# A norm's squares and the next projection's first weights, moved into the output projection ahead of it

## The chip, the cores and the metric

The kernel runs on one core of one Trainium2 chip, in one launch. The metric is the device time of the launch in microseconds. All arithmetic is in 32-bit floats; a large product is made from three matmuls over operands split into a rounded part and a rest.

## The reference, cut to what matters

The network is a block of two layers followed by a block of one layer with other branches. Every layer begins with a root-mean-square norm and a wide input projection, and its mixing part ends with an output projection added to the residual:

```python
def rms_norm(x, w):
    y = x * rsqrt(mean(x * x, axis=-1) + EPS)
    return y * w

for l in range(2):                         # first block
    h = rms_norm(x, norm_w[l]) * (1 + scale) + shift
    parts = split_in(h @ w_in[l])          # projection, then attention and two convolutions
    y = mixer_branches(parts, ...)
    x = x + gate * (y @ w_out[l])          # layer 0 also updates 256 context tokens
# second block
h = rms_norm(x, norm_mix) * (1 + scale_m) + shift_m
proj = h @ w_in                            # then Mamba, attention and gated delta branches
x = x + gate_m * (merged @ w_out)
x = x + gate_f * moe(...)
```

The model width is 1024; there are 1024 tokens and 256 context tokens (the context is dropped after the first block).

## The kernel before

The residual `k.x` stays in SBUF as 8 chunks of 128 channels (the partitions) by 1280 tokens (columns 0 to 255 are the context). `k.x_r` is the same memory, and so are `k.h` and `k.h_r`. Work is cut into stages; each ends in a barrier of all engines, and inside one the engines run their own instruction lists and wait on semaphores in them. There is no planner: the written order is the order.

An output projection is `project_residual` (L1391). It makes 8 output chunks in four groups of two, each chunk for each token block: 24 products in layer 0 (256, 512 and 512 tokens), 16 in layer 1 (512 and 512). SyncE loads the weights of a group (L1421) and the old residual from DRAM (L1430); GpSimd splits the weights of groups 1 to 3 (L1439, L1441); TensorE makes a product in 24 matmuls; VectorE adds it to `k.x` (L1516) and increments `added`, which lets TensorE use that PSUM bank in the next group. ScalarE has nothing to do after its roundings at the start (L1480, L1485).

The norm is `norm_steps` (L268), set beside the first pair of the next projection: `ring_gemm` (L392) in the first block, `delta_inputs` (L1603) behind it. It walks blocks of tokens: 512, 384 and 128 (`X_NORMS`), and in layer 1 the 256 context tokens last. SyncE loads two halves of 128 weight columns, 512 KB each (L248), then stores the residual to DRAM, one DMA for a block (L280). ScalarE squares the chunks of a block (L298), into four buffers; TensorE sums them over partitions and chunks with a matrix of ones (L287), 8 matmuls for a block; ScalarE takes Ln and Exp (L303, L307), which gives the inverse root; VectorE makes `k.h` from `k.x` (L344); ScalarE writes the rounded part over `k.x` (L314), and so waits first for the store of that block (`kept_in`); VectorE makes the rest (L350); TensorE takes the products with the two weight halves. Block 0's squares come first and those of block i + 1 are interleaved with the roundings of block i, likewise the sums between the products. The two weight halves are rounded by ScalarE (L255) and their rests made by VectorE (L262) ahead of the first block.

Products of the first pair: for the first 512 tokens both halves of the weights as each chunk arrives; for the other 512 the first half as the chunks of the 128-token block arrive, then the second half. A half of the next pair's weights is loaded when the last product that uses that half is done; ScalarE rounds it and GpSimd makes the rest (L262).

Ahead of layer 1's norm stands a small stage, `silu_columns` (L587). Ahead of the norm of `delta_inputs` there is none. Layer 0 has such a norm as well, and the mixing part's own projection in the second block is also a `project_residual`.

Of the kernel before, what the change touches and what calls it, by code (L numbers as in the profile page):

```python
# [269 lines left out]
def norm_steps(nc, k, s, norm, ring, tiles):  # L270
# [5 lines left out]
    last = len(blocks) - 1  # L276

# [4 lines left out]
    def sums(pe, i, j):  # L282
        n, w = i * DK + j, blocks[i][1]
        if i >= 2 and j == 0:
            pe.wait_ge(s.logged, i - 1)
        pe.wait_ge(s.squared, n + 1)
        nc.tensor.matmul(ps[i % 2][:, 0:w], k.ones[:, :], sq[n % 4][:, 0:w], start=j == 0, stop=j == DK - 1)\  # L287
            .then_inc(s.summed, 1)

    def scalar(act):  # L290
# [9 lines left out]
        def take_root(i):  # L300
            w = blocks[i][1]
            act.wait_ge(s.summed, (i + 1) * DK)
            nc.scalar.activation(lg[:, 0:w], ps[i % 2][:, 0:w], ACT.Ln, bias=k.eps, scale=1.0 / D).then_inc(s.logged, 1)  # L303
            act.wait_ge(s.logged, i + 1)
            if i >= 2:
                act.wait_ge(s.scaled, (i - 1) * DK)
            nc.scalar.activation(root[i % 2][:, 0:w], lg[:, 0:w], ACT.Exp, scale=-0.5).then_inc(s.rooted, 1)  # L307
# [23 lines left out]
    def vector(dve):  # L331
# [7 lines left out]
        for n in range(2):  # L339
            rest_half(nc, ring, dve, n)  # L340

        def scale(i, j):
            t0, w, which = blocks[i]
            nc.vector.scalar_tensor_tensor(k.h[:, j, t0:t0 + w], k.x[:, j, t0:t0 + w], factor[:, j, which:which + 1],  # L344
                                           root[i % 2][:, 0:w], ALU.mult, ALU.mult).then_inc(s.scaled, 1)
# [19 lines left out]
def norm_tiles(nc, es, norm):  # L365

    sq = norm.squares or [es.enter_context(sbuf(nc, f"rm_sq{i}", [P, 512], F32)) for i in range(4)]
    lg = es.enter_context(sbuf(nc, "rm_log", [P, 512], F32))
    root = [es.enter_context(sbuf(nc, f"rm_root{i}", [P, 512], F32)) for i in range(2)]
# [4 lines left out]
def ring_gemm(nc, k, name, ring, parts, blocks, then=None, extra=None, norm=None):  # L374
# [7 lines left out]
    with ExitStack() as es, stage(nc, names) as s, nc.Block() as block:  # L382
# [18 lines left out]
        def _(sp):  # L401
            if norm:
                for n in range(2):
# [23 lines left out]
        def _(pe):  # L427
# [963 lines left out]
def project_residual(nc, k, name, w, src, src_r, blocks, mod, gate_at, kept, sums=None):  # L1391
# [7 lines left out]
    names = "w_in0 w_in1 w_in2 w_in3 x_in0 x_in1 x_in2 x_in3 rounded rest w_rounded w_rest split products added summed biased"  # L1399

    with ExitStack() as es, stage(nc, names) as s, nc.Block() as block:
# [8 lines left out]
        early = DK // 2  # L1410

# [4 lines left out]
        def _(sp):  # L1416
            for g in range(n_pairs):
# [12 lines left out]
                sp.dma_start(k.x[:, pair, first:T1], kept[:, pair, first:T1]).then_inc(x_in[g], 16)  # L1430

        @block.gpsimd
        def _(pool):
            pool.wait_ge(s.rest, DK)
            for g in range(1, n_pairs):
                for c in range(2):
# [5 lines left out]
                                            ALU.subtract).then_inc(s.split, 1)  # L1442

# [33 lines left out]
        def _(act):  # L1477
# [8 lines left out]
            round_chunks(range(early, DK))  # L1486

        @block.vector
        def _(dve):
            def take_rests(chunks):  # L1490
                for j in chunks:
                    dve.wait_ge(s.rounded, j + 1)
                    nc.vector.tensor_tensor(src_r[:, j, :], src[:, j, :], k.h_r[:, j, 0:total].bitcast(F32),  # L1493
                                            ALU.subtract).then_inc(s.rest, 1)

# [12 lines left out]
            for g in range(n_pairs):  # L1508
                dve.wait_ge(x_in[g], 16)
                for t in range(per):  # L1510
# [6 lines left out]
                                                   ALU.mult, ALU.add).then_inc(s.added, 1)  # L1517

# [13 lines left out]
def first_block(nc, k, a):  # L1532
    with sbuf_views(nc, "branches", [P, DK, T1]) as (k.y, k.y_r):
        for l in range(2):
            first_layer(nc, k, a, l, l == 1)


def first_layer(nc, k, a, l, last):
# [7 lines left out]
    with ExitStack() as es, ExitStack() as conv:  # L1546
        ring = conv.enter_context(weight_ring(nc, f"ring{l}"))
# [4 lines left out]
                     weight=f"norm_w{l}", edges=edges, squares=None)  # L1552
# [7 lines left out]
        sums = attention(nc, k, a, l, last, cq, ckv, kr, ahead)  # L1560
    project_residual(nc, k, f"out{l}", a.w_out[l], k.y[:, :, blocks[0][0]:T1], k.y_r[:, :, blocks[0][0]:T1],
# [2332 lines left out]
```

## Time and profile before

| | us |
|---|---|
| median of 3 runs | 4379.31 (4378.44 to 4383.56) |
| the profiled execution | 4386.62 |
| its span | 4384.8 |
| TensorE busy | 3901.9 (89%) |
| VectorE busy | 2111.7 (48%) |
| ScalarE busy | 1575.0 (36%) |
| GpSimd busy | 617.0 (14%) |

The engines overlap, so the busy times don't add up to the span. Times of single events below count from the start of the span. The profiled execution is 7.3 us above the median. The output projection of layer 0 ends near 1137 us and layer 1's norm follows it; that of layer 1 ends near 2059 us, and the norm of `delta_inputs` follows it.

### The profile page before, as it was taken

The numbers are of one execution on the slowest core, as the hardware profiler recorded it, in microseconds if no ns is written. First come the engines' busy times: TensorE is split into PE (matmuls) and PEld (weight loads), VectorE is DVE, ScalarE is ACT, GpSimd is POOL, SyncE is SP. The second block draws the span as 40 slices with busy tenths as digits, with TensorE's granted clock in tenths as the row PEclk, the third lists the DMA queues.
The fourth block names the chain that finished last, engine by engine and source line by source line (L and its number), as shares of the span: only waits on it lengthen the run. The fifth ranks groups of instructions, "written<-read, shape, count | busy, mean of one in ns | idle before, by whom it ended". The sixth has DMA issues, their size and how long they took to land. (4 is left out here: it accounts for less than half of the span.)

```text
span 4384.8 us, 41863 instructions
## 1 busy us (share of the span) xinstructions
PE 3901.9 (89%) x16132; PEld 2780.2 (63%) x16132; DVE 2111.7 (48%) x2657; ACT 1575.0 (36%) x2450; POOL 617.0 (14%) x300
## 2 busy tenths in 40 slices
PE   4899799999899799999876889898999897999996
PEld 1687555558686455567655866576777675666664
DVE  0391366662373366651438423233343226666665
ACT  1412345541322245441452235522221114555552
POOL 0021200002021200001110011022333330111111
PEclk9999889998999799989888989999999997999997
DMA  4211100002211112122112211022233337999985
GB/s 173 77 39 32 36 15 29 29 29 91 68 44 41 31 53 63 58 80 93 30 20 68 49 40 20 10 72 78 82 94 77 89 121 257 360 352 353 354 293 211
DMA packets 339924, 450.95 MB, mean 103 GB/s; under 512 B 45149, under 2 KB 214418, under 8 KB 338194
## 3 DMA queue, kind: packets, MB, share of 16 engines
q1 hardware_dynamic: 325026, 405.30, 29.5%
q0 software_dynamic: 12112, 25.19, 1.6%
q10 hardware_dynamic: 2592, 17.83, 1.0%
q8 instruction: 128, 2.10, 0.2%
q14 instruction: 66, 0.54, 0.0%
HBM read 408.41 MB, written 59.24 MB: 107 GB/s over the span
## 5 line engine op out<-in xcount | busy, mean ns | idle before, releaser
L1140 PE MATMUL values<-probs,vp 128*128 128x512 f32 x672 | 349.0, 601 | 12.0 <-issue 6.4
L1228 ACT ACTIVATE probs<-scores 128x512 f32<-128x512 f32 (+1 forms) x336 | 196.0, 583 | 307.9 <-PE scores L220 306.2
L218 PE MATMUL scores<-q_hi,k_rest 97*128 97x512 f32 (+1 forms) x336 | 262.4, 781 | 0.0
L3555 PE MATMUL dp<-h_t,abt 128*128 128x512 f32 x544 | 241.9, 597 | 1.1 <-ACT abt L3604 0.9
L3586 ACT ACTIVATE expert_hi<-wu 128x1024 fp32r<-128x1024 f32 x136 | 144.8, 1065 | 250.6 <-PE gp L220 250.6
L1309 DVE TENSOR_REDUCE mx<-made 128x1 f32<-128x640 f32 (+1 forms) x272 | 203.9, 794 | 28.7 <-PE made L1081 27.9
L218 PE MATMUL gates_ps<-x_t_r,ring_r 128*128 128x512 f32 (+1 forms) x560 | 206.2, 368 | 2.6 <-PEq L84 2.6
L218 PE MATMUL smb<-x_t_r,merge_w_r 128*128 128x512 f32 x480 | 195.9, 408 | 13.9 <-POOL merge_w_r L2802 11.1
L730 DVE SCALAR_TENSOR_TENSOR conv_out<-conv_in,vectors,conv_out 128x1295 f32<-128x1295 f32 (+1 forms) x120 | 205.5, 1713 | 4.3
L219 PE MATMUL gates_ps<-h_t_r,ring_hi 128*128 128x512 f32 (+1 forms) x560 | 206.1, 368 | 0.0
L220 PE MATMUL gates_ps<-x_t_r,ring_hi 128*128 128x512 f32 (+1 forms) x560 | 206.0, 368 | 0.0
L3637 DVE TENSOR_TENSOR wu_r<-wu,expert_hi 128x1024 fp32r<-128x1024 f32 x136 | 166.4, 1225 | 74.3 <-ACT expert_hi L3586 71.4
L1439 POOL TENSOR_TENSOR out_hi<-out_w,ones 128x1024 fp32r<-128x1024 f32 x18 | 43.0, 2392 | 1076.9 <-DVE branches_r L1493 947.3
L220 PE MATMUL smb<-x_t_r,merge_hi 128*128 128x512 f32 x480 | 192.4, 401 | 0.0
L262 POOL TENSOR_TENSOR ring_r<-ring_w,ring_hi 128x1024 fp32r<-128x1024 f32 x40 | 104.9, 2623 | 550.1 <-ACT ring_hi L255 550.1
L218 PE MATMUL out_ps<-h_t_r,out_w_r 128*128 128x512 f32 (+1 forms) x448 | 171.1, 382 | 10.9 <-DVE out_w_r L1499 10.9
L3637 DVE TENSOR_TENSOR wg_r<-wg,expert_hi 128x1024 fp32r<-128x1024 f32 x136 | 165.7, 1225 | 21.1 <-ACT expert_hi L3586 13.4
L3555 PEld LDWEIGHTS dp<-h_t,abt 128*128 128x128 f32 x544 | 100.6, 190 | 117.6 <-issue 114.8
L3052 DVE TENSOR_TENSOR merge_sg<-smb,merge_sg 128x512 f32<-128x512 f32 x48 | 33.2, 692 | 287.1 <-PE smb L220 287.1
L220 PE MATMUL out_ps<-h_t_r,out_hi 128*128 128x512 f32 (+1 forms) x448 | 170.1, 380 | 0.0
L1516 DVE SCALAR_TENSOR_TENSOR x_t<-out_ps,mod,x_t 128x512 f32<-128x512 f32 (+1 forms) x56 | 39.1, 711 | 250.3 <-PE out_ps L220 250.2
L1140 PEld LDWEIGHTS values<-probs,vp 128*128 128x128 f32 x672 | 111.2, 190 | 74.9 <-issue 42.7
(572 smaller groups left out, 9525.9 us busy)
## 6 DMA issues: line engine op xcount, KB each, us to landing
wg<-in_w_gate SPq DMA_DIRECT2D x34, 2048.0 KB, 10.0
wu<-in_w_up SPq DMA_DIRECT2D x34, 2048.0 KB, 11.2
h_t<-in_w_down SPq DMA_DIRECT2D x34, 2048.0 KB, 9.7
ahead_w<-in_w_ada SPq DMA_DIRECT2D x48, 512.0 KB, 3.9
ring_w<-in_w_in SPq DMA_DIRECT2D x44, 512.0 KB, 4.1
mod_w<-in_w_mod ACTq DMA_DIRECT2D x8, 1536.0 KB, 29.2
ahead_w<-in_w_mod SPq DMA_DIRECT2D x24, 512.0 KB, 3.5
out_w<-in_w_out SPq DMA_DIRECT2D x24, 512.0 KB, 4.9
```

The lines of the kernel that those rows point to most:

```text
L218: nc.tensor.matmul(out, lhs[1], rhs[0], start=start, stop=False, **kw)
L219: nc.tensor.matmul(out, lhs[0], rhs[1], start=False, stop=False, **kw)
L220: return nc.tensor.matmul(out, lhs[0], rhs[0], start=False, stop=stop, **kw)
L262: eng.tensor_tensor(ring.rest[:, c, :, :], ring.w[:, c, :, :], ring.hi[:, c, :, :].bitcast(F32), ALU.subtract)\
L730: step(nc.vector.scalar_tensor_tensor(o, i, wt, o, ALU.mult, ALU.add))
L1140: nc.tensor.matmul(O[b % 2][:, 0:w], vp[g // 2 % 2][:, kb, g % 2 * VD:g % 2 * VD + P], pr[m % 3][:, 0:w], start=kb == 0, stop=kb == nk - 1 ...
L1228: nc.scalar.activation(pr[m % 3][:, 0:w], S[m % 2][:, 0:w], ACT.Exp, scale=scale).then_inc(s.exped, 1)
L1309: nc.vector.tensor_reduce(mx[:, p, j:j + 1], src, AX.X, ALU.max).then_inc(s.maxed, 1)
L1439: nc.gpsimd.tensor_tensor(hi[:, q, :, :], wt[:, q, :, :], all_ones(k), ALU.mult).then_inc(s.split, 1)
L3555: m = nc.tensor.matmul(dp[half][:, :], at[:, j, :], wd[u][:, j, half * 512:(half + 1) * 512], start=j == 0, stop=j == FK - 1)
L3586: nc.scalar.activation(w_hi[:, p % RING, :, :], weights(u, p, False), ACT.Copy).then_inc(s.w_hi, 1)
L3637: nc.vector.tensor_tensor(weights(u, p, True), weights(u, p, False), w_hi[:, p % RING, :, :].bitcast(F32), ALU.subtract).then_inc(s.w_rest, 1)
```

## The change

- `project_residual` gets `ahead` for the two layers of the first block: the weight ring of the next projection, its first columns, and a buffer `summed` of 128 by 1280 (5 KB a partition, at a fixed place). Behind its other DMAs SyncE loads the two first halves. After each `added`, ScalarE squares that piece of `k.x` and VectorE adds it to `summed`, one product later. ScalarE rounds the two halves ahead of the first square of the last group, and GpSimd makes their rests behind its other work.
- In the norms of layer 1 and of `delta_inputs`, one matmul with the ones for a token block takes the place of eight and of the squares; ScalarE takes all roots first, in buffers that hold every token; the loads, roundings and rests of the first two halves are gone from there.
- The ring is opened ahead of `project_residual` and closed where it was closed (in `delta_branch` for the last). Layer 0's norm and the third `project_residual` do what they did.

```diff
@@ norm_steps
+    summed, fresh = norm.summed, ring.halves == 0
+    sums_each = 1 if summed is not None else DK
...
+        if summed is not None:
+            if j == 0:
+                nc.tensor.matmul(ps[i % 2][:, 0:w], k.ones[:, :], summed[:, t0:t0 + w], start=True, stop=True)\
+                    .then_inc(s.summed, 1)
+            return
...
+            act.wait_ge(s.summed, (i + 1) * sums_each)
+            r = root[i % len(root)][:, 0:w]
+            log = r if lg is None else lg[:, 0:w]
+            nc.scalar.activation(log, ps[i % 2][:, 0:w], ACT.Ln, bias=k.eps, scale=1.0 / D).then_inc(s.logged, 1)
...
-        for j in range(DK):
-            square(0, j)
-        round_half(nc, ring, act, 0)
+        if summed is None:
+            for j in range(DK):
+                square(0, j)
+        if fresh:
+            round_half(nc, ring, act, 0)
         take_root(0)
-        round_half(nc, ring, act, 1)
+        if fresh:
+            round_half(nc, ring, act, 1)
+        if summed is not None:
+            for i in range(1, len(blocks)):
+                take_root(i)
         for i in range(len(blocks)):
             for j in range(DK):
-                if i < last and j < DK // 2:
+                if summed is None and i < last and j < DK // 2:
                     square(i + 1, 2 * j)
                     square(i + 1, 2 * j + 1)
-                if i < last and j == 6:
+                if summed is None and i < last and j == 6:
                     take_root(i + 1)
                 round_chunk(i, j)
...
-        for n in range(2):
-            rest_half(nc, ring, dve, n)
+        if fresh:
+            for n in range(2):
+                rest_half(nc, ring, dve, n)
@@ ring_gemm
         @block.sync
         def _(sp):
             if norm:
-                for n in range(2):
+                for n in range(split_before, 2):
                     load_half(sp, ring, n, parts[0][1](0))
                 steps.store(sp)
...
-                for j in range(DK):
-                    steps.sums(pe, 0, j)
+                for i in range(1 if norm.summed is None else len(norm.blocks)):
+                    for j in range(DK):
+                        steps.sums(pe, i, j)
                 for i, (t0, w, _) in enumerate(norm.blocks):
                     here = [b for b in range(nb) if blocks[b][0] + blocks[b][1] == t0 + w]
                     for j in range(DK):
-                        if i + 1 < len(norm.blocks) and j < DK // 2:
+                        if norm.summed is None and i + 1 < len(norm.blocks) and j < DK // 2:
                             steps.sums(pe, i + 1, 2 * j)
                             steps.sums(pe, i + 1, 2 * j + 1)
@@ project_residual
+            if ahead:
+                for n in range(2):
+                    load_half(sp, ring, n, ring_columns)
...
+            if ahead:
+                for n in range(2):
+                    rest_half(nc, ring, pool, n)
...
@@ project_residual, ScalarE and VectorE
+            if ahead:
+                for n in range(n_pairs * per):
+                    g, t = divmod(n, per)
+                    c, b = divmod(t, nb)
+                    t0, w_, _ = blocks[b]
+                    if n == (n_pairs - 1) * per:
+                        for h in range(2):
+                            round_half(nc, ring, act, h)
+                    if n >= nb + 2:
+                        act.wait_ge(s.totalled, n - nb - 1)
+                    act.wait_ge(s.added, n + 1)
+                    to = total_sq[:, t0:t0 + w_] if n < nb else sq[n % 2][:, 0:w_]
+                    nc.scalar.activation(to, k.x[:, 2 * g + c, t0:t0 + w_], ACT.Square).then_inc(s.squared, 1)
...
+
+            def add_square(n):
+                t0, w_, _ = blocks[n % nb]
+                dve.wait_ge(s.squared, n + 1)
+                if n >= 2 * nb:
+                    dve.wait_ge(s.totalled, n - 2 * nb + 1)
+                total = total_sq[:, t0:t0 + w_]
+                nc.vector.tensor_tensor(total, total, sq[n % 2][:, 0:w_], ALU.add).then_inc(s.totalled, 1)
...
+                    if ahead and g * per + t > nb:
+                        add_square(g * per + t - 1)
+            if ahead:
+                add_square(n_pairs * per - 1)
@@ first_layer
+    conv = ExitStack()
+    ring = conv.enter_context(weight_ring(nc, f"ring{l + 1}"))
+    summed = nc.alloc_sbuf_tensor_at(f"summed{l}", [P, T1], F32, offset=SUMMED_AT)
+    columns = cols_of(a.w_in_2[0], C_GQKV, 0) if last else cols_of(a.w_in[1], C_CF, 0)
     project_residual(nc, k, f"out{l}", a.w_out[l], k.y[:, :, blocks[0][0]:T1], k.y_r[:, :, blocks[0][0]:T1],
-                     blocks, mod, 2 * DK, k.kept, sums)
+                     blocks, mod, 2 * DK, k.kept, sums, (ring, columns, summed))
+    ring.halves = 2
+    return conv, ring, summed
```

## Rows read from the trace of the kernel before

**Rows 1.** The page's busy times: engine, busy us, share of the span, instructions.
```profile
PE 3901.9 (89%) x16132; PEld 2780.2 (63%) x16132; DVE 2111.7 (48%) x2657; ACT 1575.0 (36%) x2450; POOL 617.0 (14%) x300
```

**Rows 2.** Timeline of VectorE at layer 1's norm: start, us, instruction, count, idle before and releaser.
```profile
1136.08 0.75 DVE L1516 SCALAR_TENSOR_TENSOR x_t<-out_ps,mod,x_t 128x512 f32<-128x512 f32 x1 [4.69 <-PE out_ps L220]
...
1189.91 0.87 DVE L344 SCALAR_TENSOR_TENSOR h_t<-x_t,rm_factor,rm_root 128x256 f32<-128x256 f32 x2
```

**Rows 3.** The same of ScalarE.
```profile
1137.44 1.28 ACT L587 ACT_TABLE_LOAD   x1 [123.69 <-PEq L84]
...
1139.64 1.28 ACT L291 ACT_TABLE_LOAD   x1 [0.60 <-PEq L84]
1140.93 2.19 ACT L298 ACTIVATE conv_out<-x_t 128x512 f32<-128x512 f32 x4
...
1156.06 0.72 ACT L314 ACTIVATE x_t_r<-h_t,mod 128x512 fp32r<-128x512 f32 x1 [1.20 <-DVE h_t L344]
...
1197.75 1.07 ACT L255 ACTIVATE ring_hi<-ring_w 128x1024 fp32r<-128x1024 f32 x1
```

**Rows 4.** The same of SyncE: DMA issues; the us are the sequencer's.
```profile
1081.36 0.58 SPq L1430 DMA_DIRECT2D x_t<-x_kept  x1
...
1140.68 11.62 SPq L280 DMA_DIRECT2D x_kept<-x_t  x4
1191.54 68.06 SPq L248 DMA_DIRECT2D ring_w<-in_w_in  x7
```

**Rows 5.** The same of TensorE.
```profile
1201.29 0.50 PE L218 MATMUL cf_ps<-x_t_r,ring_r 128*128 128x512 f32 x1 [4.34 <-POOL ring_r L262]
```

**Rows 6.** DMA issues at layer 1's norm: tile, queue, count, size, median us from issue to landing.
```profile
ring_w<-in_w_in SPq DMA_DIRECT2D x9, 512.0 KB, 4.1
x_kept<-x_t SPq DMA_DIRECT2D x1, 2048.0 KB, 10.0
```

**Rows 7.** Timeline of VectorE at the norm of delta_inputs.
```profile
2078.21 0.75 DVE L350 SCALAR_TENSOR_TENSOR h_t_r<-h_t,mod,x_t_r 128x512 fp32r<-128x512 f32 x1 [2.25 <-ACT x_t_r L314]
...
2084.96 0.75 DVE L350 SCALAR_TENSOR_TENSOR h_t_r<-h_t,mod,x_t_r 128x512 fp32r<-128x512 f32 x1 [2.45 <-ACT x_t_r L314]
...
2097.27 0.62 DVE L350 SCALAR_TENSOR_TENSOR h_t_r<-h_t,mod,x_t_r 128x384 fp32r<-128x384 f32 x1 [1.45 <-ACT x_t_r L314]
...
2103.68 0.35 DVE L350 SCALAR_TENSOR_TENSOR h_t_r<-h_t,mod,x_t_r 128x128 fp32r<-128x128 f32 x1 [0.27 <-ACT x_t_r L314]
...
2122.53 3.11 DVE L1796 TENSOR_SCALAR branches<-gdn_held,vectors 128x1024 f32<-128x1024 f32 x2 [14.52 <-ACT gdn_held L1756]
...
2153.64 1.42 DVE L1796 TENSOR_SCALAR branches<-gdn_held,vectors 128x1024 f32<-128x1024 f32 x2 [20.83 <-ACT gdn_held L1756]
```

**Rows 8.** The same of ScalarE.
```profile
2059.40 1.28 ACT L291 ACT_TABLE_LOAD   x1 [99.55 <-PEq L84]
...
2077.46 0.72 ACT L314 ACTIVATE x_t_r<-h_t,mod 128x512 fp32r<-128x512 f32 x1 [3.25 <-DMA x_kept<-x_t]
```

**Rows 9.** The same of TensorE.
```profile
2104.09 0.79 PE L218 MATMUL gdn_ps<-x_t_r,gdn_r 128*128 128x512 f32 x1 [5.89 <-DVE h_t_r L350]
...
2124.49 0.80 PE L218 MATMUL gdn_ps<-x_t_r,gdn_r 128*128 128x512 f32 x1 [6.38 <-POOL gdn_r L262]
```

**Rows 10.** The same of SyncE.
```profile
2112.70 65.01 SPq L248 DMA_DIRECT2D gdn_w<-in_w_in  x6
```

**Rows 11.** DMA issues at the norm of delta_inputs.
```profile
x_kept<-x_t SPq DMA_DIRECT2D x1, 2048.0 KB, 17.0
```

**Rows 12.** Stretches there: busy us of PE, PEld, DVE, ACT, POOL, then TensorE's granted clock.
```profile
2104.00:2108.00 4.00, 3.91 (x9) 3.14 (x10) 3.82 (x15) 2.98 (x8) 0.00 (x0) 0.50 0.01 2
```

**Rows 13.** Timeline of GpSimd there.
```profile
2122.09 2.34 POOL L262 TENSOR_TENSOR gdn_r<-gdn_w,gdn_hi 128x1024 fp32r<-128x1024 f32 x1 [98.78 <-ACT gdn_hi L255]
```

**Rows 14.** The page's row of a 512-column addition on VectorE.
```profile
L3052 DVE TENSOR_TENSOR merge_sg<-smb,merge_sg 128x512 f32<-128x512 f32 x48 | 33.2, 692 | 287.1 <-PE smb L220 287.1
```

**Rows 15.** Landing of the residual's loads in the two projections: min, median, max us.
```profile
DMA to landing us min/median/max: 6.1/7.1/8.3
```

More of the change, by code:

```diff
@@ L365, in norm_tiles @@
 def norm_tiles(nc, es, norm):
-    sq = norm.squares or [es.enter_context(sbuf(nc, f"rm_sq{i}", [P, 512], F32)) for i in range(4)]
-    lg = es.enter_context(sbuf(nc, "rm_log", [P, 512], F32))
-    root = [es.enter_context(sbuf(nc, f"rm_root{i}", [P, 512], F32)) for i in range(2)]
+    sq = norm.squares
+    if norm.summed is None:
+        lg = es.enter_context(sbuf(nc, "rm_log", [P, 512], F32))
+        root = [es.enter_context(sbuf(nc, f"rm_root{i}", [P, 512], F32)) for i in range(2)]
+    else:
+        lg, whole = None, es.enter_context(sbuf(nc, "rm_roots", [P, T1], F32))
+        root = [whole[:, t0:t0 + w] for t0, w, _ in norm.blocks]
     ps = [es.enter_context(psum(nc, f"rm_ps{i}", [P, 512], F32)) for i in range(2)]
@@ L1398, in project_residual @@
     total = T1 - first
-    names = "w_in0 w_in1 w_in2 w_in3 x_in0 x_in1 x_in2 x_in3 rounded rest w_rounded w_rest split products added summed biased"
+    names = "w_in0 w_in1 w_in2 w_in3 x_in0 x_in1 x_in2 x_in3 rounded rest w_rounded w_rest split products added summed biased squared totalled"
     with ExitStack() as es, stage(nc, names) as s, nc.Block() as block:
@@ L1410, in project_residual @@
         early = DK // 2
+        if ahead:
+            ring, ring_columns, total_sq = ahead
+            sq = [es.enter_context(sbuf(nc, f"{name}_sq{i}", [P, 512], F32)) for i in range(2)]
+            assert nc.sbuf_base <= SUMMED_AT and SUMMED_AT + 4 * T1 <= nc.sbuf_top
         def place(g, c):
@@ L1609, in delta_inputs @@
     per, steps, n_ch = 2 * nb, 2 * TAPS, 2 * PAIRS
-    norm = named(blocks=X_NORMS, mod=k.mods[2], shift_at=0, scale_at=DK, weight="norm_mix")
+    norm = named(blocks=X_NORMS, mod=k.mods[2], shift_at=0, scale_at=DK, weight="norm_mix", summed=summed)
     names = ("products evacuated conv_steps silu_done qk_squared qk_summed qk_logged qk_rooted qk_scaled "
              "loaded small_rounded small_rest wide_made wide_kept turned x_step act_step" + NORM_NAMES)
-    with ExitStack() as es, weight_ring(nc, "gdn") as ring, stage(nc, names) as s, nc.Block() as block:
+    with ExitStack() as es, stage(nc, names) as s, nc.Block() as block:
         def sb(n, shape, dt=F32):
@@ L1645, in _ @@
         def _(sp):
-            for n in range(2):
-                load_half(sp, ring, n, cols_of(w_in, C_GQKV, 0))
             first.store(sp)
@@ L1681, in sum_squares @@
                 last.then_inc(s.qk_summed, 1)
-            for j in range(DK):
-                first.sums(pe, 0, j)
+            for i in range(len(X_NORMS)):
+                first.sums(pe, i, 0)
             for i, (t0, w, _) in enumerate(X_NORMS):
@@ L1687, in _ @@
                 for j in range(DK):
-                    if i + 1 < len(X_NORMS) and j < DK // 2:
-                        first.sums(pe, i + 1, 2 * j)
-                        first.sums(pe, i + 1, 2 * j + 1)
                     for b in here:
@@ L3762, in _, with second_block @@
                 sp.wait_ge(stored[b], 16 * (NT2 // 2))
-def second_block(nc, k, a, out):
+def second_block(nc, k, a, out, ahead):
     r = named()
```

45 lines of the change are left out of this document (23 added, 22 removed).

## The prediction, made before the changed kernel was run

> **What bounds the kernel now.** I read the page first: TensorE is busy 89% of the span [rows 1], so what a change off TensorE can win lies in the stretches where TensorE waits. Then came the timelines of the engines around the two norms that the change touches: layer 1's, call it A, and that of `delta_inputs`, B. Both show one picture. Up to the last product of the output projection TensorE works without a gap, VectorE adds 0.75 us of work to every 5.44 us (its row says 4.69 idle and 0.75 busy) and ScalarE does nothing for some 100 us [rows 2, 3, 8]. Then the stage ends and TensorE lives from hand to mouth: ScalarE squares eight chunks [rows 3], the roots follow, and VectorE's rests (L350) hand TensorE one chunk after another. The end of interest is the first matmul of the second pair of weights, behind which TensorE is again full: 1201.29 in A, 2124.49 in B [rows 5, 9]. What I work out is how much earlier that matmul comes. All stages behind it start from barriers and keep their length, so the gain is carried to the end.
>
> What sets that matmul, read backwards: GpSimd's rest of the half, ScalarE's rounding, the weights' load, and the last product that used the half (the load is issued then, 1191.54 and 2112.70 [rows 4, 10]); that product waits for the rests of the 128-token block, and those for the whole walk of VectorE and ScalarE over the 512 and 384 tokens ahead. The walk begins with the first L314: 1156.06 in A, where VectorE's h had just come from the root, and 2077.46 in B, where the store of block 0 was the last to come [rows 3, 8]. So B's walk already waits for the store, and the squares hide behind it; in A the store (10.0 us from 1140.68, thus 1150.7) is 5.4 us earlier than the walk [rows 4, 6].
>
> **What is added ahead of the norm.** 24 squares in layer 0's projection and 16 in layer 1's, and about as many additions. A square of 512 columns I take at 0.63 us (four took 2.19 in a row, [rows 3], and longer alone), an addition at 0.69, like the one row of that kind [rows 14]. ScalarE has no other work; VectorE has 4.69 idle us for each product and TensorE needs an `added` only a group later, so they cost nothing but at the end: behind the last update (L1516, which ends at 1136.83 in A [rows 2]) come one square and one addition that nothing covers, with two semaphores 1.4 us in each projection. Bounds: 0.7 (were the square hidden) and 2.5 (each half as long again). The two loads go out behind SyncE's last residual load, 1081.36 in A [rows 4]; they have till about 1109 before ScalarE wants them, and even a landing as late as the longest store here would fit, so loads, two roundings (1.07 each) and two GpSimd rests are hidden by the projection's last products. If that cover were gone, ScalarE would hold its squares, but the last group of TensorE's products waits only for the group before; the end would slip from some 45 us of landing on.
>
> One rule speaks against the additions. A row first: two L1796 of VectorE took 3.11 us where GpSimd ran L262 beside them and 1.42 where it did not [rows 7, 13]. The Trainium skill, page "SBUF — State Buffer", section "SBUF: two separate sides", says that VectorE and GpSimd share a port pair that one of them holds for its whole instruction, also where VectorE has two SBUF inputs against a GpSimd op that reads SBUF; an addition of the squares is such an op. The trace agrees in that the pair of L1796 came 1.69 us later. By it an addition may stand up to the 2.34 us of one GpSimd op, 3.03 in all, still under the 4.69 idle; at the end of the stage GpSimd is done, so the sum stays.
>
> **What goes, A.** The stage starts 1.4 later, 1141.0 for 1139.64 (the start of ScalarE's table load, [rows 3]; the silu stage between keeps its length). From it go two weight loads, 32 squares, 28 of 32 summing matmuls, two roundings and two rests. Roots: table load to 1142.3, then four pairs of Ln and Exp of at most 0.69 + 0.63 for 512 columns, one behind another: done by about 1147.6 if all were of 512 columns, sooner as they are. VectorE has its first two h by 1145.5. Now the store is late: SyncE issues it first. Before, 3 MB (two halves and block 0) were down 11.1 us after the start (1139.6 to 1150.7). Without 1 MB of weights I take 8.4 us: 3 MB in 11.1 with some 2 us of start and end is about 2.7 to 3 us a MB. Bounds: 7.1 (the median of the residual's loads, 1 to 1.3 MB each [rows 15]) and 10.0 (unchanged [rows 6]); below about 7 the roots would be the later ones. So L314 at 1149.4 and the first rest 0.75 later, as in B [rows 7, 8], 1150.2.
>
> The walk: in B it took from 2078.21 (first rest) to 2104.09 (TensorE's first matmul on the second 512 tokens) 25.9 us. In it VectorE stood 2.45, 1.90 and 1.45 us for ScalarE, which each time stood in a square or a root that waited for summing matmuls (three such rows; the first and the last are in [rows 7]): those three go, 5.8 us, and 20.1 stay. (Bounds: 25.9 if the waits only change their name; 18.6, my estimate, if VectorE's 32 steps followed each other with no wait at all.) TensorE can't hold this walk: its products of the first 512 tokens need 8 times 6 matmuls, 11 us at full clock and under 20 at half. So TensorE starts on the second 512 at 1170.3. It comes to this from an idle stretch, at the low level of its clock: in B the granted clock there was 0.50, that is 1.2 GHz, and the first half took from 2104.09 to 2112.70, 8.6 us for 24 matmuls [rows 9, 10, 12]. I keep the 8.6: 1178.9. (With the low level throughout, 24 times the 0.43 us between two starts, it were 10.2.) The load lands after 4.1 [rows 6], 1183.0. ScalarE must be free by then: the context block's walk took from 1189.91 to the rounding at 1197.75, 7.8 us with the first evacuations [rows 2, 3]; it now begins some 4.2 us behind 1170.1, the first rest of the 128-token block (eight rests and as many h of 0.35 us at most [rows 7], overlapping), so it ends at 1182.1, just in time. Rounding to first matmul: 1197.75 to 1201.29, 3.5 us. Result 1186.5 against 1201.29: 14.8 us earlier.
>
> **What goes, B.** Start 2059.40 + 1.4 = 2060.8 [rows 8]; store 8.4 (before, 17.0 from its issue [rows 11], behind two halves of w_in that landed slowly, and these are gone); L314 at 2069.2, first rest 2070.0, walk 20.1, 2090.1; first half 8.6, 2098.7; load, rounding and rest as before, 2124.49 − 2112.70 = 11.8 [rows 9, 10], 2110.5. Against 2124.49: 14.0 us. Upper bound of the store here 17.0, which leaves nothing of its part.
>
> **Sum.** 14.8 + 14.0 = 28.8 us. The profiled execution was 4386.62, so it would be 4357.8; it lay 7.3 above the median of the runs, and from that median, 4379.31, the forecast is 4350.5.
>
> **Rivals.**
> 1. The store stays as slow as it was: 10.0 in A (1.6 lost) and 17.0 in B (8.6 lost). For it: writing to DRAM had the same queues, and B's number is large. Against: 1 MB ahead of it goes, and B's weights alone took longer than A's. 28.8 − 10.2 = 18.6, 4360.7.
> 2. The walk keeps its 25.9: the stalls were put down to the wrong releaser and come back as waits between VectorE and ScalarE. For it: L314 needs h and L350 needs L314, one after the other. Against: a stall of 0.15 to 0.3 us is all that the other rows of that walk show. 28.8 − 11.6 = 17.2, 4362.1. Both 1 and 2: 7.0 left, 4372.3, within what counts as no change.
> 3. The other side: the squares make VectorE the bound of the projections. Its list is in order: an addition that waits for its square (or for GpSimd's port, the rule above) has the next L1516 behind it, and TensorE waits for that `added` a group later. Place: all 40 products; the price is what update and addition take together above 5.44 us for each. It decides from 4.7 us an addition on; at 5.4 the gain is eaten, and at 5.7 it costs 40 us, so 4390. The rows say 0.7 to 3.
>
> **How the numbers follow.** Forecast 0.76 (its own range 4343 to 4357: stores from 7.1 to 10, tails, a clock that stays high at the end), rival 1 0.08, rival 2 0.08, both 0.05, rival 3 0.03. A measurement of this kernel tells about 0.2%, 8.8 us, from no change. Faster 0.92, same 0.05, slower 0.03. Range 4341 to 4363: it takes in rivals 1 and 2 alone and leaves out the rest.
>
> **What would show it.** In the profile after: VectorE's last addition about 1.4 us behind the last L1516 and TensorE without new gaps in both projections; the first rounding of the norm released by the store, 8.4 us behind the stage's start; no wait of ScalarE on summing matmuls inside the walk, and 20 us from the first rest to TensorE's second 512 tokens; then the second pair's first matmul 14 to 15 us earlier in each. A store over 12 us, a walk over 23 us or a gap between products of the projections would make it wrong.

## The result, and the profile after

| | before | changed |
|---|---|---|
| first measurement, median | 4381.44 (4378.44 to 4385.11, 4 runs) | 4356.50 (4350.08 to 4361.99, 4 runs) |
| second measurement, median | 4377.30 (4371.50 to 4384.77, 19 runs) | 4350.16 (4345.18 to 4354.15, 5 runs) |
| span of the profiled execution | 4384.8 | 4360.2 |

The ratio is 0.9942 (95% interval 0.9925 to 0.9959) in the first and 0.9933 (0.9920 to 0.9946) in the second: 25 and 29 us. The forecast was 28.8 us less, 4350.5, with a range of 4341 to 4363; 4356.5 lies in it. (It started from 4379.31, the median of the first three runs of before; with a fourth run that median is 4381.44, and the measured gain 24.9 us.)

The measure for the two norms is one stretch: from the start of VectorE's last L1516 of a projection (L1568 in the changed file) to the first matmul with the second pair of weights. I call it the gap stretch; A is layer 1's norm, B that of `delta_inputs`, as ahead.

| gap stretch, us | A | B |
|---|---|---|
| before, first profile | 65.2 | 66.6 |
| before, second profile | 65.2 | 63.2 |
| changed, first profile | 49.0 | 50.4 |
| changed, second profile | 49.0 | 50.2 |

Before, A runs from 1136.08 to 1201.29 [rows 2, 5], and B from 2057.94, the last update of layer 1's projection, to 2124.49 [rows 9]:

```profile
2057.94 0.75 DVE L1516 SCALAR_TENSOR_TENSOR x_t<-out_ps,mod,x_t 128x512 f32<-128x512 f32 x1 [4.69 <-PE out_ps L220]
```

The timelines of the changed kernel for the same engines follow; columns as in [rows 2]. VectorE in A, whose first row answers to the last update of [rows 2]:

```profile
1136.49 0.75 DVE L1568 SCALAR_TENSOR_TENSOR x_t<-out_ps,mod,x_t 128x512 f32<-128x512 f32 x1 [4.36 <-PE out_ps L220]
1137.16 0.68 DVE L1546 TENSOR_TENSOR summed<-summed,out_sq 128x512 f32<-128x512 f32 x1
1138.00 0.69 DVE L1546 TENSOR_TENSOR summed<-summed,out_sq 128x512 f32<-128x512 f32 x1 [0.16 <-ACT out_sq L1530]
...
1149.66 0.75 DVE L366 SCALAR_TENSOR_TENSOR h_t_r<-h_t,mod,x_t_r 128x512 fp32r<-128x512 f32 x1 [3.13 <-ACT x_t_r L323]
```

ScalarE in A, answering to [rows 3]:

```profile
1141.53 1.28 ACT L298 ACT_TABLE_LOAD   x1 [0.63 <-PEq L84]
1143.66 0.69 ACT L312 ACTIVATE rm_roots<-rm_ps,eps 128x512 f32<-128x512 f32 x1 [0.84 <-PE rm_ps L290]
...
1147.02 0.42 ACT L316 ACTIVATE rm_roots<-rm_roots 128x256 f32<-128x256 f32 x1
1148.90 1.33 ACT L323 ACTIVATE x_t_r<-h_t,mod 128x512 fp32r<-128x512 f32 x2 [1.47 <-DMA x_kept<-x_t]
...
1181.93 1.06 ACT L255 ACTIVATE ring_hi<-ring_w 128x1024 fp32r<-128x1024 f32 x1 [0.87 <-DMA ring_w<-in_w_in]
```

TensorE in A, answering to [rows 5]:

```profile
1141.57 3.45 PE L290 MATMUL rm_ps<-summed,ones 128*128 128x512 f32 x6 [5.12 <-PEq L84]
...
1150.46 0.79 PE L218 MATMUL cf_ps<-x_t_r,ring_r 128*128 128x512 f32 x1 [4.24 <-DVE h_t_r L366]
...
1169.46 0.79 PE L218 MATMUL cf_ps<-x_t_r,ring_r 128*128 128x512 f32 x1 [5.81 <-DVE h_t_r L366]
...
1185.46 0.76 PE L218 MATMUL cf_ps<-x_t_r,ring_r 128*128 128x512 f32 x1 [2.09 <-POOL ring_r L262]
```

SyncE in A, answering to [rows 4], and then the DMA view, answering to [rows 6]:

```profile
1141.53 9.41 SPq L282 DMA_DIRECT2D x_kept<-x_t  x4
1177.97 54.83 SPq L248 DMA_DIRECT2D ring_w<-in_w_in  x6
```

```profile
x_kept<-x_t SPq DMA_DIRECT2D x1, 2048.0 KB, 7.4
```

Three things are to be seen. The stage starts at 1141.53, which is 5.0 us behind the start of the last update, where it was 3.6 before (1136.08 to 1139.64): behind the update stand the addition of the square before (1137.16), which was ready, and the last one (1138.00), which waited 0.16 us for its square. The roots are done at 1147.44 (1147.02 + 0.42), and the first rounding still stands 1.47 us for `DMA x_kept<-x_t`: the store is the last to come, 7.4 us behind its issue. Then 19.8 us pass from the first rest (1149.66) to TensorE's first matmul on the second 512 tokens (1169.46), without one wait for a summing matmul.

B is the same picture. VectorE, ScalarE, TensorE and the DMA view, answering to [rows 7], [rows 8], [rows 9] and [rows 11]:

```profile
2041.26 0.75 DVE L1568 SCALAR_TENSOR_TENSOR x_t<-out_ps,mod,x_t 128x512 f32<-128x512 f32 x1 [4.09 <-PE out_ps L220]
...
2052.50 0.75 DVE L366 SCALAR_TENSOR_TENSOR h_t_r<-h_t,mod,x_t_r 128x512 fp32r<-128x512 f32 x1 [4.11 <-ACT x_t_r L323]
```

```profile
2044.22 1.28 ACT L298 ACT_TABLE_LOAD   x1 [1.49 <-PEq L84]
...
2051.74 1.33 ACT L323 ACTIVATE x_t_r<-h_t,mod 128x512 fp32r<-128x512 f32 x2 [3.26 <-DMA x_kept<-x_t]
```

```profile
2072.30 0.79 PE L218 MATMUL gdn_ps<-x_t_r,ring_r 128*128 128x512 f32 x1 [5.02 <-DVE h_t_r L366]
...
2091.66 0.79 PE L218 MATMUL gdn_ps<-x_t_r,ring_r 128*128 128x512 f32 x1 [6.24 <-POOL ring_r L262]
```

```profile
x_kept<-x_t SPq DMA_DIRECT2D x1, 2048.0 KB, 7.5
```

The store took 17.0 us before and takes 7.5 now, and the rounding still waits for it (3.26 us).

### The profile page after: what moved, and what is told of

Read it like the earlier page. It is cut to its first block and busy times, and to the rows that moved or that the text cites. A ratio compares the mean times of both kernels' runs of the same rounds, so it can differ in the third digit from the quotient of the medians.

```text
span 4360.2 us, 41746 instructions
## 1 busy us (share of the span) xinstructions
PE 3873.7 (89%) x16034; PEld 2766.1 (63%) x16034; DVE 2133.7 (49%) x2688; ACT 1577.7 (36%) x2434; POOL 626.2 (14%) x304
## 5 line engine op out<-in xcount | busy, mean ns | idle before, releaser
L262 POOL TENSOR_TENSOR ring_r<-ring_w,ring_hi 128x1024 fp32r<-128x1024 f32 x54 | 142.3, 2638 | 744.6 <-ACT ring_hi L255 744.6
L3699 DVE TENSOR_TENSOR wg_r<-wg,expert_hi 128x1024 fp32r<-128x1024 f32 x136 | 165.7, 1225 | 21.1 <-ACT expert_hi L3648 13.4
L1102 PE MATMUL made<-k_hi,q_hi 96*128 96x512 f32 (+2 forms) x528 | 128.2, 360 | 32.5 <-ACT k_hi L1212 16.5
## 6 DMA issues: line engine op xcount, KB each, us to landing
wg<-in_w_gate SPq DMA_DIRECT2D x34, 2048.0 KB, 10.1
h_t<-in_w_down SPq DMA_DIRECT2D x34, 2048.0 KB, 10.1
```

Source lines behind the costliest of these rows:

```text
L262: eng.tensor_tensor(ring.rest[:, c, :, :], ring.w[:, c, :, :], ring.hi[:, c, :, :].bitcast(F32), ALU.subtract)\
L1102: x = nc.tensor.matmul(out[:, c:c + w], q_hi[g % 2][0:QK, j * P:(j + 1) * P], k_hi[g % 2][0:QK, keys], start=True, stop=True)
L3699: nc.vector.tensor_tensor(weights(u, p, True), weights(u, p, False), w_hi[:, p % RING, :, :].bitcast(F32), ALU.subtract).then_inc(s.w_rest, 1)
```

## The experiments

Each kernel is compared with the kernel before on its own chip; the first, third, fourth and fifth of them shared one, the others another. What a kernel wins in a gap stretch is taken against the mean of the two profiles of before, 65.2 in A and 64.9 in B.

**The changed kernel again (changed_again).** No edit.

> The changed kernel once more, for its time against the kernel before and for a second profile. In the first profile the two norms had won 33 us by 2151 us of the span, and 8 of these were gone at the end of the span (24.6 us left). Theory (chance): the second half of the program, with its transfers of expert weights, takes a few us more or less in each execution; then the second profile again shows 32 to 33 us at 2151, and at the end any value from 24 to 38; the median is 25 to 33 us under before. Rival (the change costs something later): the second profile loses the same 8 us behind 2151, and all medians stay near 25.

4350.16 us, 27.1 under the median of before, by the ratio 29 (24 to 35). The gap stretches are 49.0 (1137.27 to 1186.30) and 50.2 (2042.13 to 2092.32), those of the first profile to 0.2 us. At B's second pair this profile is 32.2 us ahead of the first of before (2092.32 for 2124.49), and at the end of the span 32.5 us (4352.3 for 4384.8), where the first profile of the changed kernel was 24.6 shorter. From B's second pair to the end it took 2260.0 us; the first profile of the changed kernel took 2268.5, and the seven other profiles of this text 2256.9 to 2260.3. So the 8 us are not a cost of the change; they are the difference of two executions of one kernel. Against the second profile of before (span 4375.2) the two spans of the changed kernel are only 15.0 and 22.9 us shorter: single spans can't size this gain.

**The kernel before again (before_again).** No edit.

> The kernel before once more, timed against itself and profiled a second time. In the two norms the first profile of the changed kernel and the second one are 32.4 us shorter from the last update of the projections to the second pair's first matmul, yet the medians were 25 and 27 us apart. Theory (chance in the other stages): the second profile of before shows the same 65.2 and 66.6 us there, and shifts of 3 to 8 us against the first profile elsewhere, of both signs; its median against itself lies within 3 us. Rival (the stretches themselves vary, and 32 us is a lucky pair): the two stretches of this profile differ from those of the first by more than 2 us.

4377.20 us against 4376.21, ratio 1.0004 (0.9994 to 1.0015). Its profile has a span of 4375.2 for 4384.8: 9.6 us between two executions of one kernel. The expectation of equal stretches held in A (65.2, 1133.18 to 1198.40) and failed in B, which took 63.2 (2055.07 to 2118.27) for 66.6, so that there the rival was right. B's rows of this profile, ScalarE, the DMA view, VectorE and TensorE:

```profile
2073.42 0.72 ACT L314 ACTIVATE x_t_r<-h_t,mod 128x512 fp32r<-128x512 f32 x1 [2.92 <-DMA x_kept<-x_t]
```

```profile
x_kept<-x_t SPq DMA_DIRECT2D x1, 2048.0 KB, 15.8
```

```profile
2074.17 0.75 DVE L350 SCALAR_TENSOR_TENSOR h_t_r<-h_t,mod,x_t_r 128x512 fp32r<-128x512 f32 x1 [1.92 <-ACT x_t_r L314]
```

```profile
2098.28 0.79 PE L218 MATMUL gdn_ps<-x_t_r,gdn_r 128*128 128x512 f32 x1 [5.89 <-DVE h_t_r L350]
```

The store landed after 15.8 us for 17.0, and the first rounding still waited for it (2.92 us): that is 1.2 of the 3.4 us. Another 1.8 are the walk, from the first rest to TensorE's second 512 tokens: 24.1 us (2074.17 to 2098.28) for 25.9. In the first profile the granted clock was 0.50 in the four us in which TensorE took up the walk (2076 to 2080), here 0.86 (2072 to 2076), and the first wait of VectorE, 2.45 us there [rows 7], is 0.67 here. The last 0.4 lie behind the walk. So the first profile of before showed B about 1.7 us longer than the mean, and its gain that much larger.

**Only the squares ahead (squares_only).** The weights are loaded, rounded and split in the norm.

```diff
-            if ahead:
-                for n in range(2):
-                    load_half(sp, ring, n, ring_columns)
...
-            if ahead:
-                for n in range(2):
-                    rest_half(nc, ring, pool, n)
...
-                    if n == (n_pairs - 1) * per:
-                        for h in range(2):
-                            round_half(nc, ring, act, h)
...
-    ring.halves = 2
...
+            for n in range(2):
+                load_half(sp, ring, n, cols_of(w_in, C_GQKV, 0))
```

> Squares and sums made ahead in the projection, but the two weight halves loaded, rounded and split in the norm as before. Theory (the store of the first block starts the walk, and what is ahead of it in the queue sets when it lands): the first rounding comes about 11 us behind the start of the stage in A and 17 to 18 in B, for 7.4 and 7.5 in the changed kernel, so that 3.6 us of the gain go in A and 10 in B; the walks keep the 19 us of the changed kernel; 14 us slower than the changed kernel. Rival (the weights ahead of the store cost nothing, the squares are all): as fast as the changed kernel.

4364.92 us (4358.55 to 4373.90), ratio 0.9970 (0.9959 to 0.9980), 12.4 us under before and some 15 behind the changed kernel, for 14 expected. ScalarE in A and in B, and B's landing:

```profile
1140.05 1.28 ACT L298 ACT_TABLE_LOAD   x1 [0.60 <-PEq L84]
...
1151.18 1.33 ACT L323 ACTIVATE x_t_r<-h_t,mod 128x512 fp32r<-128x512 f32 x2 [1.15 <-DMA x_kept<-x_t]
```

```profile
2043.37 1.28 ACT L298 ACT_TABLE_LOAD   x1 [1.49 <-PEq L84]
...
2060.79 1.33 ACT L323 ACTIVATE x_t_r<-h_t,mod 128x512 fp32r<-128x512 f32 x2 [2.43 <-DMA x_kept<-x_t]
```

```profile
x_kept<-x_t SPq DMA_DIRECT2D x1, 2048.0 KB, 16.4
```

From the start of the stage the first rounding comes after 11.1 us in A and 17.4 in B (7.4 and 7.5 in the changed kernel), both times released by the store, as foretold (11, and 17 to 18). The walks keep 19.8 us in both. The gap stretches are 52.8 (1135.04 to 1187.86) and 60.3 (2040.41 to 2100.67), 3.8 and 10.0 us longer than in the changed kernel for 3.6 and 10 expected. The rival, that weights ahead of the store cost nothing, is out.

**Only the weights ahead (weights_only).**

```diff
+                        act.wait_ge(s.added, n)
...
-                    if n >= nb + 2:
-                        act.wait_ge(s.totalled, n - nb - 1)
-                    act.wait_ge(s.added, n + 1)
-                    to = total_sq[:, t0:t0 + w_] if n < nb else sq[n % 2][:, 0:w_]
-                    nc.scalar.activation(to, k.x[:, 2 * g + c, t0:t0 + w_], ACT.Square).then_inc(s.squared, 1)
...
-                    if ahead and g * per + t > nb:
-                        add_square(g * per + t - 1)
-            if ahead:
-                add_square(n_pairs * per - 1)
...
-    return conv, ring, summed
+    return conv, ring, None
...
-        tiles = (None, None, [rt[:, 0, t0 - CTX:t0 - CTX + w] for t0, w, _ in X_NORMS],
+        tiles = ([sq[:, i // 2, 512 * (i % 2):512 * (i % 2 + 1)] for i in range(4)], rt[:, 1, 0:512],
+                 [rt[:, 0, 0:512], rt[:, 0, 512:]],
...
-            for i in range(len(X_NORMS)):
-                first.sums(pe, i, 0)
+            for j in range(DK):
+                first.sums(pe, 0, j)
...
+                    if i + 1 < len(X_NORMS) and j < DK // 2:
+                        first.sums(pe, i + 1, 2 * j)
+                        first.sums(pe, i + 1, 2 * j + 1)
```

> Weights loaded and split ahead in the projection, squares and sums in the norm as before; the projections end without the 1.45 us of a last square and addition. Theory: in A the walk waits for squares and roots and begins only 1 us earlier than before; in B it begins some 5 us earlier, when roots and not the store are last; the walk stays at 25.9 us in both, as the sums stand in it. Together 6 us faster than before, 26 slower than the changed kernel; with squares_only this does not add up to the whole, because each part alone leaves the other wait in place. Rival (each part has its own share): the gains of the two kernels with one part add up to that of both, near 32 us in the two norms.

4369.33 us (4365.41 to 4374.13), ratio 0.9982 (0.9973 to 0.9991), 8.0 us under before. ScalarE in A and in B:

```profile
1138.89 1.28 ACT L298 ACT_TABLE_LOAD   x1 [0.60 <-PEq L84]
...
1153.41 0.72 ACT L323 ACTIVATE x_t_r<-h_t,mod 128x512 fp32r<-128x512 f32 x1
```

```profile
2055.55 1.28 ACT L298 ACT_TABLE_LOAD   x1 [20.48 <-PEq L84]
...
2068.71 0.72 ACT L323 ACTIVATE x_t_r<-h_t,mod 128x512 fp32r<-128x512 f32 x1
```

The first rounding has no wait in brackets: roots and h, not the store, are last, 14.5 us behind the start in A (16.4 before) and 13.2 in B (18.1 before), so 1.9 and 4.9 us earlier for 1 and 5 expected. The walks took 24.2 and 24.1 us (1154.17 to 1178.38, 2069.46 to 2093.57), not the 25.9 expected; 25.9 was the one walk of before at the low clock. The gap stretches are 62.6 (1135.33 to 1197.96) and 59.5 (2054.04 to 2113.53), 8.0 us less than the mean of before, for 6 expected. With the squares' 12.4 and 4.6 us that makes 25.0, and the changed kernel has 30.8: the parts don't add up. Cut at the first rest and at TensorE's second 512 tokens, the stretches show where they don't (us; before is the mean of two profiles, changed the first):

| | A: to the first rest | walk | behind | B: to the first rest | walk | behind |
|---|---|---|---|---|---|---|
| before | 20.7 | 24.3 | 20.2 | 19.7 | 25.0 | 20.2 |
| squares_only | 16.9 | 19.8 | 16.1 | 21.1 | 19.8 | 19.3 |
| weights_only | 18.8 | 24.2 | 19.6 | 15.4 | 24.1 | 20.0 |
| changed | 13.2 | 19.8 | 16.0 | 11.2 | 19.8 | 19.4 |

The walk is shortened by the squares alone, and so is most of what follows it in A. Ahead of the walk the two parts win 5.7 us in A and 2.9 in B, and both together 7.5 and 8.5, because each alone leaves the other wait standing there: with the squares alone B even reaches its first rest 1.4 us later, since the store still comes last and the stage starts later. By the medians it is 12.4 + 8.0 = 20.4 against 27.1.

**Additions four times as long (adds_four).**

```diff
-    names = "w_in0 w_in1 w_in2 w_in3 x_in0 x_in1 x_in2 x_in3 rounded rest w_rounded w_rest split products added summed biased squared totalled"
+    names = "w_in0 w_in1 w_in2 w_in3 x_in0 x_in1 x_in2 x_in3 rounded rest w_rounded w_rest split products added summed biased squared totalled again"
...
-                total = total_sq[:, t0:t0 + w_]
-                nc.vector.tensor_tensor(total, total, sq[n % 2][:, 0:w_], ALU.add).then_inc(s.totalled, 1)
+                total, one = total_sq[:, t0:t0 + w_], sq[n % 2][:, 0:w_]
+                for r in range(3):
+                    nc.vector.tensor_tensor(one, one, one, ALU.max).then_inc(s.again, 1)
+                    dve.wait_ge(s.again, 3 * (n - nb) + r + 1)
+                nc.vector.tensor_tensor(total, total, one, ALU.add).then_inc(s.totalled, 1)
```

> The changed kernel with three more passes of VectorE over each square (a maximum with itself, same values) ahead of its addition, so that an addition takes four times its 0.69 us. Theory (additions are hidden, but the last two are not): TensorE has no new gap between the products of the projections; the stage after each projection starts 4 us later (2 additions, of which the one before the last was hidden), 8 us slower in all than the changed kernel. Rival (VectorE's list is what binds the projections): 40 additions of 2.1 us more each, up to 80 us slower.

VectorE at the end of the projection in B, and TensorE's second pair there:

```profile
2038.27 0.75 DVE L1571 SCALAR_TENSOR_TENSOR x_t<-out_ps,mod,x_t 128x512 f32<-128x512 f32 x1 [1.91 <-PE out_ps L220]
2038.93 2.14 DVE L1547 TENSOR_TENSOR out_sq<-out_sq 128x512 f32<-128x512 f32 x3
2041.11 0.69 DVE L1549 TENSOR_TENSOR summed<-summed,out_sq 128x512 f32<-128x512 f32 x1
2041.72 2.14 DVE L1547 TENSOR_TENSOR out_sq<-out_sq 128x512 f32<-128x512 f32 x3
2043.89 0.69 DVE L1549 TENSOR_TENSOR summed<-summed,out_sq 128x512 f32<-128x512 f32 x1
```

```profile
2091.87 0.80 PE L218 MATMUL gdn_ps<-x_t_r,ring_r 128*128 128x512 f32 x1 [6.05 <-POOL ring_r L262]
```

The norm's stage starts 4.1 us later in each, for 4 expected, and the gap stretches grew by 3.8 us in A (52.8, 1136.44 to 1189.22) and by 3.3 in B (53.6, 2038.27 to 2091.87). The view of waits names no wait of TensorE between the products of the projections, with single or with fourfold additions, and from its first to its last matmul layer 0's projection took 112.8 us before, 112.8 in the changed kernel and 112.7 here. (There are 35 additions in the two projections, not 40: the first square of a token block is written and not added.) So even 2.8 us for an addition is hidden but at the end, and rival 3 is out at this size; beside GpSimd's rests two additions took 4.9 and 4.6 us with their extra passes, and TensorE didn't wait for these either. That additions bind when all of them take 4.7 us was not tried. The median, 4351.64 (4348.30 to 4365.41), is only 1.5 us above the changed kernel's where the stretches say 7. In the profile the part between the two stretches took 849.1 us here and 855.8 in both profiles of the changed kernel, which is as large and of the other sign; why it is shorter is open. The intervals (0.9932 to 0.9960, and 0.9920 to 0.9946) overlap, and a loss of 7 us can't be told from none with so few runs.

**The residual stored inside the projection (stores_early).**

```diff
-        s = es.enter_context(stage(nc, "ring_in0 ring_in1 ring_rounded ring_rest"))
+        s = es.enter_context(stage(nc, "ring_in0 ring_in1 ring_rounded ring_rest ring_stored"))
...
-                    pairs=0, halves=0)
+                    pairs=0, halves=0, stored=s.ring_stored, pieces=0)
...
+        if ring.pieces:
+            return
...
-                act.wait_ge(kept_in[i], 16)
+                act.wait_ge(ring.stored if ring.pieces else kept_in[i], 16 * (ring.pieces or 1))
...
+                for g in range(n_pairs - 1):
+                    sp.wait_ge(s.added, (g + 1) * per)
+                    sp.dma_start(kept[:, 2 * g:2 * g + 2, first:T1], k.x[:, 2 * g:2 * g + 2, first:T1])\
+                        .then_inc(ring.stored, 16)
+                for t in range(per):
+                    c, b = divmod(t, nb)
+                    t0, w_, _ = blocks[b]
+                    n = DK - 2 + c
+                    sp.wait_ge(s.added, (n_pairs - 1) * per + t + 1)
+                    sp.dma_start(kept[:, n:n + 1, t0:t0 + w_], k.x[:, n:n + 1, t0:t0 + w_]).then_inc(ring.stored, 16)
+                ring.pieces = n_pairs - 1 + per
```

> The changed kernel, with the residual stored to DRAM inside the projection: three pieces of two chunks, then the last products one by one, so that the norm has only the last 256 KB to wait for. Theory (the store of the first block, 7.4 us after the start, is what releases the walk): the first rounding then follows the last root, 5.9 us behind the start in A and 4.4 in B, so 1.5 and 3.1 us earlier; 4 to 5 us faster than the changed kernel, and no wait on the store is left. Rival (the wait on the store hides another, such as h from VectorE): the first rounding comes no earlier and the time stays.

4342.21 us (4337.04 to 4346.09) against 4376.21 on that chip, ratio 0.9917 (0.9904 to 0.9931): 34 us under before, some 7 beyond what the changed kernel won on the other chip. ScalarE in A and in B:

```profile
1148.80 1.32 ACT L325 ACTIVATE x_t_r<-h_t,mod 128x512 fp32r<-128x512 f32 x2
```

```profile
2043.78 1.32 ACT L325 ACTIVATE x_t_r<-h_t,mod 128x512 fp32r<-128x512 f32 x2
```

The rounding has no wait now and comes 5.9 and 4.2 us behind the start of the stage, for 5.9 and 4.4 expected. The gap stretches are 46.7 (1137.93 to 1184.67) and 47.9 (2036.24 to 2084.16), 2.3 and 2.4 us less than in the changed kernel. Together 4.7 us, for 4 to 5 expected: the store did release the walk. The median is 34.0 us under before for 27.1 in the changed kernel, and the stretches account for 4.7 of these 7; the intervals of the two ratios overlap, so the medians alone don't show the difference.

**Two of the roots put into the walk as well (stores_roots).**

```diff
-            for i in range(1, len(blocks)):
-                take_root(i)
+            take_root(1)
...
+                if summed is not None and i == 0 and 2 <= j + 1 < len(blocks):
+                    take_root(j + 1)
```

> As stores_early, and only the roots of the first two blocks are taken ahead; those of the third and fourth stand between roundings of the first block. Theory: the first rounding follows the first h, about 4.5 us behind the start in A and 3.7 in B, 3 and 3.8 us earlier than in the changed kernel; each later root may hold the walk for 0.3 us; 6 us faster than the changed kernel. Rival: the roots in the walk give back what the earlier start wins, and it is no faster than stores_early.

4342.09 us (4340.44 to 4346.73), ratio 0.9921 (0.9908 to 0.9935): the time of stores_early. The gap stretches, 45.7 (1134.61 to 1180.35) and 47.1 (2035.99 to 2083.11), are 1.0 and 0.8 us shorter, and the first rounding follows the first h. TensorE in A of stores_early and of this kernel:

```profile
1150.34 0.80 PE L218 MATMUL cf_ps<-x_t_r,ring_r 128*128 128x512 f32 x1 [2.66 <-DVE h_t_r L368]
...
1169.33 0.79 PE L218 MATMUL cf_ps<-x_t_r,ring_r 128*128 128x512 f32 x1 [4.99 <-DVE h_t_r L368]
...
1184.67 0.50 PE L218 MATMUL cf_ps<-x_t_r,ring_r 128*128 128x512 f32 x1 [2.24 <-POOL ring_r L262]
```

```profile
1145.61 0.50 PE L218 MATMUL cf_ps<-x_t_r,ring_r 128*128 128x512 f32 x1 [1.30 <-DVE h_t_r L369]
...
1164.60 0.79 PE L218 MATMUL cf_ps<-x_t_r,ring_r 128*128 128x512 f32 x1 [6.20 <-DVE h_t_r L369]
...
1180.35 0.80 PE L218 MATMUL cf_ps<-x_t_r,ring_r 128*128 128x512 f32 x1 [2.05 <-POOL ring_r L262]
```

From TensorE's first matmul of the walk to that of the second 512 tokens it is 18.99 us in both, so the roots cost nothing in the walk, against the rival. Against the changed kernel the stretches are 3.3 and 3.2 us shorter, 6.5 for the 6 expected. The medians can't tell the 1.8 us between this kernel and stores_early, so which of the two is faster stays open there; that both are faster than the changed kernel rests on the stretches.

## Why the prediction was right, step by step

**The tail.** One square and one addition, 1.4 us later in each. Measured: from the start of the last update to the start of the stage 5.04 us for 3.56 in A, thus 1.5; in B 2.96 (2041.26 to 2044.22) for 1.46 (2057.94 to 2059.40 [rows 8]), thus 1.5 too. The size was right and the order inside was not: the addition of the square before stands between, and it hides the last square for all but 0.16 us. What is added is two additions and this 0.16, not a square and an addition; that the two sums are alike is luck.

**The cover in the projections.** Right: no wait of TensorE between their products, also with fourfold additions. One addition of layer 0's projection met GpSimd's rests. VectorE and GpSimd there:

```profile
1109.60 0.68 DVE L1546 TENSOR_TENSOR summed<-summed,out_sq 128x512 f32<-128x512 f32 x1
...
1112.28 2.11 DVE L1546 TENSOR_TENSOR summed<-summed,out_sq 128x512 f32<-128x512 f32 x1
1117.27 0.75 DVE L1568 SCALAR_TENSOR_TENSOR x_t<-out_ps,mod,x_t 128x512 f32<-128x512 f32 x1 [2.89 <-PE out_ps L220]
```

```profile
1111.43 5.20 POOL L262 TENSOR_TENSOR ring_r<-ring_w,ring_hi 128x1024 fp32r<-128x1024 f32 x2 [21.16 <-ACT ring_hi L255]
```

The addition took 2.11 us for 0.68, and GpSimd's two rests 5.20 us together, where the same two took 4.76 in weights_only, which has no additions. It stayed hidden: 2.89 us of idle time were left ahead of the next update. The Trainium skill ("SBUF — State Buffer", section "SBUF: two separate sides") states that a VectorE operation with two SBUF inputs and a GpSimd operation that reads SBUF don't share their port pair: the second is blocked until the first is done. This trace agrees: the addition ended at 1114.39, some 0.6 us behind the first rest (1111.43 and 2.4 us). The rows of L1796 that the prediction took for it are of another operation; this one is the addition itself.

**The store.** 8.4 us were taken and 7.4 and 7.5 measured, still last, with the roots 1.5 us ahead in A (the rounding waited 3.3 us in B). This is the term that was too dear, by 1.0 us in A and 0.9 in B. Squares_only shows the whole mechanism: the same DMA lands 11 and 17 us behind the start when 1 MB of weights goes out ahead of it. Rival 1 is out.

**The walk.** 20.1 us foretold, 19.8 measured in A and in B. The three stalls went with the summing matmuls; rival 2 is out. But 25.9 and 5.8 us are the size of one case, B in the first profile: before, A's walk took 24.3 us in both profiles with stalls of 0.76, 1.90 and 1.46, B's second one took 24.1, and so did both in weights_only, where the sums stay. What the sums cost is thus 4.3 to 4.5 us, and another 1.8 in that one walk, whose first products ran at the low clock. The 20.1 came right because the stalls were taken off the walk in which they stood. One bound was wrong: 48 products at the low level are 48 times 0.43, some 20.5 us and not under 20, so TensorE could have held a walk that ran wholly at that level. It didn't: in A it stood idle for 5.81 us ahead of the second 512 tokens.

**Behind the walk.** Half of the products and the load's start: 8.5 us in A (1169.46 to 1177.97) for 8.6; from there to the second pair 7.5 for 7.6. In B 7.7 us (to 2080.02) and 11.6 for 8.6 and 11.8: the 0.9 us are the clock, which rose sooner: the two stretches behind TensorE's start, answering to [rows 12],

```profile
2072.00:2076.00 4.00, 3.70 (x9) 2.92 (x10) 3.82 (x15) 2.92 (x9) 0.00 (x0) 0.50 0.00 0
2076.00:2080.00 4.00, 4.00 (x18) 3.26 (x17) 0.23 (x2) 0.81 (x2) 0.00 (x0) 0.95 0.00 0
```

show 0.50 and then 0.95, where before the second four us had 0.73:

```profile
2108.00:2112.00 4.00, 4.00 (x14) 3.14 (x14) 0.02 (x1) 0.59 (x2) 0.00 (x0) 0.73 0.00 0
```

**The sum.** Against the first profile of before the stretches shrank by 16.2 and 16.2 us for 14.8 and 14.0 foretold; against the mean of both profiles of before 30.8 (16.2 and 14.6). The medians say 25 and 27, with intervals that reach 35. The 4 to 6 us between medians and stretches are found in no part that the change touches: the part between the stretches took 856.7 us in both profiles of before and 855.8 in both of the changed kernel, the part behind them is given under changed_again, and the start of layer 0's projection, ahead of all that was changed, lay anywhere from 1020.0 to 1024.6 us in the nine profiles. So they may be chance; that is not shown. Mechanism and size held. What was too sure was the single profile as the base: its B was 3.4 us longer than that of the next, and its span 9.6. Against that next profile B's gain is 12.8 us, under the 14.0 foretold, where against the first it is 16.2.

## What to carry to other kernels

- Where a stage begins with a transfer that something must wait for, look at what is issued ahead of it on that queue: here 1 MB of weights held a 2 MB store from 7.4 to 11 us in one place and 17 in another.
- Two waits ahead of the same step pay in full only when both go: in B, ahead of the walk, the parts won 2.9 us and the whole 8.5. Once both are gone the next one (here the store itself) is worth a look; taking it away gave 4.7 us more in the stretches.
- A change of some 5 us in 4380 can be read from a stretch in the profile, but not from the medians of a few runs, nor from two spans. Take the profile of before twice: A repeated to 0.1 us, and B, which hung on a slow landing and on the clock, moved by 3.4.

## What the runs showed that was not expected

- Two executions of one kernel differ by 8 to 10 us in their spans (4384.8 and 4375.2 before; 4360.2 and 4352.3 changed), while the stretch in A repeated to 0.1 us in both kernels.
- The landing of one 2 MB store was within 7.3 to 7.5 us in each of eight stretches (four profiles, of three kernels) where nothing stood ahead of it, and 15.8, 16.4 and 17.0 in B with two halves of weights ahead, for 10.0 and 10.1 in A with halves of the same size. B's halves themselves land slowly: 9.0 to 9.7 us in the median for 4.8 to 5.0 in A when two go out together, and 8.2 us for 4.1 when one goes alone (2112.70 and 1191.54, before). Why those columns land slower was not tried.
